# The second block's phase tables written one operation at a time along two loops, and lower halves of the down projection that alternate between VectorE and GpSimd

## The chip, the cores and the metric

The kernel runs on one core of a Trainium2 chip. The metric is the device time of one execution in microseconds. The kernel before took 1963.02 us (median of 3 runs, 1962.67 to 1963.16).

## What is computed

Two transformer-like blocks, one after the other, on a sequence of 256 tokens with 1024 features, all in float32. The first block has two layers. Each is a mixing part (three kinds of attention) and a gated MLP with a short convolution:

```python
def conv_gated_mlp(h, w_up, conv_w, conv_b, w_down):
    u = h @ w_up                      # 1024 -> 2 x 2816
    u = lax.conv_general_dilated(u, conv_w[:, None, :], window_strides=(1,),
                                 padding=[(CONV_WIDTH - 1, 0)], ...) + conv_b
    gate, val = jnp.split(u, 2, axis=-1)
    return (jax.nn.silu(gate) * val) @ w_down
```

The second block has a state space branch (a complex scan over time in 32 groups), a sparse attention, gates and a mixture of 16384 small experts:

```python
def second_block(x, ...):
    xn = rmsnorm(h, norm1_g[layer])
    proj = xn @ w_in[layer]
    y_ssm = s5_branch(u, a_re[layer], a_im[layer], log_dt[layer], ...)
    ...
```

The kernel does the complex scan as a real one, after turning each step by a phase. For that it needs tables of sine and cosine of phase times time, 16 groups of 128 states by 256 steps each. These are the phase tables of the title. Their argument depends on the weights alone, not on the sequence.

## The kernel before

**Split products.** A float32 product is done in three matmuls: each operand is split into an upper half (rounded to fp32r, `hh`, `wh`, `yh`, `ach`) and a lower half (the rest, `hl`, `wl`, `yl`, `acl`), and high x high, high x low and low x high are added in PSUM (`mm3`, line 468).

**Units of weights.** All weights come in units of 128 x 1024 float32, in one list `plan`, in the order of use. Unit i goes through `raw` (a transfer, issued from the SyncE queue), `wh` (ScalarE, line 845) and `wl` (VectorE, line 1121, or GpSimd, line 1709), each with six buffers in this part of the kernel. The transfer of unit i waits for the lower half of unit i - 6; the upper half waits for TensorE to be done with unit i - 6. Which engine writes a unit's lower half is decided by the list `lower` (lines 218 to 241). In the up projections it goes by threes, VectorE, VectorE, GpSimd ("ddp"), up to the sixth last of their units; the last five alternate. In the down projections the first 14 of 22 units are GpSimd's and the last 8 VectorE's.

**Order of the work.** Every engine has its own program, written out by hand (`pe`, `act`, `dve`, `pool`), and waits on the others by semaphores. `stream(i)`, called in each of them at the same places, does all units up to five beyond i. One layer's MLP is:

- the up loop, 22 steps. Step f has units 2f (gate half) and 2f + 1 (value half) of the up weights, 24 matmuls each, and one PSUM bank. All engines stream these two units, which means that ScalarE makes the upper halves of units 2f + 5 and 2f + 6 and VectorE or GpSimd their lower halves. Then ScalarE copies the gate half with scale and bias into a buffer of `att` (`cb`), VectorE adds the two shifted terms of the convolution (line 1138, two instructions of one element a cycle that read PSUM and `att`), ScalarE applies Silu and copies the value half, VectorE does that one's convolution, GpSimd multiplies the two (line 1714, att<-att), ScalarE rounds the previous product to `yh`, GpSimd writes its rest `yl`.
- the down loop, 22 units, 12 matmuls of 512 columns each: two groups of tokens by two halves of the output, in four banks that collect all 22. It needs y of f for unit f.

**Phase tables.** `phase_tables(L)` (line 1252) makes the arguments of half of the tables in each layer L, 4 pairs of groups by sine and cosine. VectorE calls it once, between the two loops (line 1402). It has 36 instructions on tiles of 128 x 512, all with operands in SBUF, each of them waiting for the one before: a product of time and frequency, for the cosine a quarter added, then the nearest integer found by adding and subtracting a large constant in a scratch tile `ptmp`, and subtracted. The scratch tile lies in `att`, in buffers of the convolution, so the function first waits for GpSimd's last `yl`. ScalarE turns the arguments into sines in later parts of the kernel.

```python
                for f in range(NTILE):
                    stream(first["wup", L] + 2 * f)
                    stream(first["wup", L] + 2 * f + 1)
                    ...
                phase_tables(L)
                for f, t in down_order:
                    if t:
                        stream(first["wdown", L] + f)
```

Of the kernel before, what the change touches and what calls it, by code (L numbers as in the profile page):

```python
# [26 lines left out]
NTILE = 22  # L27
# [61 lines left out]
def tcols(t):  # L89
    return slice(t * 128, (t + 1) * 128)  # L90
# [5 lines left out]
def program(nc, x_d, pos_d, consts_d, smalls_d, win_d, wout_d, wup_d, wdown_d, rows_d, wu_d, wqkv_d, wqk_d, wga_d, wsm_d,  # L96
            wglu_d, wsu_d, wau_d, wout2_d, wpq_d, keys_d, ut_d, vt_d, out_d, spill_d):
    with ExitStack() as ctx:

        def scoped(where, name, n, dt=F32):  # L100
            return where.enter_context(nc.sbuf_tensor(name, [128, n], dt))
# [17 lines left out]
        att = scoped(sc_l, "att", 3072)[:, :]  # L119
        headtmp = scoped(sc_l, "headtmp", 512)[:, :]  # L120
# [29 lines left out]
        def signal(name, step=1):  # L150
            return Signal(ctx.enter_context(nc.semaphore(name)), name, step)

        pe_out, act_out, dve_out, pool_out = [signal(n) for n in ("pe_out", "act_out", "dve_out", "pool_out")]
# [8 lines left out]
        plan, first = [], {}  # L162
# [54 lines left out]
        lower = []  # L217
        for i in range(n_units):
            d2 = first["wga"] - 8 <= i < first["wglu"] - 2
            if first["ut"] <= i < first["ut"] + J_GATE:  # L220
                lower.append("p")
            elif first["ut"] <= i < first["vt"]:
                lower.append("d")
            elif i >= first["ut"]:
                lower.append("dp"[i % 2])
            elif i >= first["wpq"]:
                lower.append("dp"[i % 2])
            elif i >= first["wglu"] - 2:
                lower.append("p")
            elif d2:  # L230
                lower.append("d")
            else:
                L = 0 if i < first["row", "n", 1] else 1
                if first["row", "n", L] + 7 <= i < first["wdown", L] - 5 and not (L == 0 and i < first["win", 0] + 6):
                    lower.append("ddp"[i % 3])
                elif first["wdown", L] <= i < first["wdown", L] + 14:
                    lower.append("p")
                elif first["wdown", L] + 14 <= i < first["wdown", L] + NTILE:
                    lower.append("d")
                else:  # L240
                    lower.append("dp"[i % 2])

        def raw_of(i):
            return raws[slot[i]][:, 0:plan[i][1]]

        def high_of(i):
            return whs[slot[i]][:, 0:plan[i][1]]

        def low_of(i):
            return wls[slot[i]][:, 0:plan[i][1]]  # L250
# [24 lines left out]
        def con(c, n):  # L275
            return con_s[:, c - 128:c - 128 + n]
# [136 lines left out]
        def ps(*item):  # L413
            return banks[bank_of[item]][:, :]

        def quad(bank, n=4):
            return bank[:, 0:n * 128].rearrange("p (k c) -> p k c", k=n)
# [694 lines left out]
        def dve(v):  # L1112
            at = [0]

            def stream(i):
                while at[0] <= until[i]:
                    u = at[0]
                    at[0] += 1
                    if plan[u][2] and lower[u] == "d":
                        v.wait_ge(act_hi, ("hi", u))  # L1120
                        v.e.tensor_tensor(low_of(u), raw_of(u), high_of(u).bitcast(F32), ALU.subtract).then_inc(dve_lo.up(("lo", u)), 1)  # L1121


            def tt(out, a, b, op, ev=None, alone=False):
                if not alone:
                    v.wait_ge(dve_out)
                v.e.tensor_tensor(out, a, b, op).then_inc(dve_out.up(ev), 1)  # L1127

            def ts(out, a, s1, s2, op0, op1, ev=None):
                v.wait_ge(dve_out)  # L1130
                if op1 is None:
                    v.e.tensor_scalar(out, a, s1, None, op0).then_inc(dve_out.up(ev), 1)  # L1132
                else:
                    v.e.tensor_scalar(out, a, s1, s2, op0, op1).then_inc(dve_out.up(ev), 1)

            def stt(out, a, s, b, op0, op1, ev=None):
                v.wait_ge(dve_out)
                v.e.scalar_tensor_tensor(out, a, s, b, op0, op1).then_inc(dve_out.up(ev), 1)  # L1138
# [23 lines left out]
            def halves_low(k0, n, cols, src, hi, ev):  # L1162
                v.wait_ge(act_out, hi)
                tt(hTl[:, k0:k0 + n, cols], src, hTh[:, k0:k0 + n, cols].bitcast(F32), ALU.subtract, ev, alone=True)

            def turned(st, ts_, nq, k_off=0):
                for t in ts_:
                    for q in range(nq):
                        halves_low(k_off + 4 * q, 4, tcols(t), quad(ps("T", st, t, q)), ("hTh", st, t, q), ("hT", st, t, q))
# [35 lines left out]
            def state_constants():  # L1205
# [43 lines left out]
                tt(kr, t16[1], t16[0], ALU.mult)  # L1249
                tt(ki, t16[2], t16[0], ALU.mult)  # L1250

            def phase_tables(L):
                ptmp = att[:, 0:512].rearrange("p (n t) -> p n t", n=2)
                tv = con(K_T, 256).unsqueeze(1).broadcast_to([128, 2, 256])
                v.wait_ge(pool_out, ("y", L, NTILE - 1))
                for n in range(8 * L, 8 * L + 8, 2):
                    fb = fr[:, n:n + 2].unsqueeze(2).broadcast_to([128, 2, 256])
                    for tab, quarter in ((sinT, 0.0), (cosT, 0.25)):
                        o = tab[:, n:n + 2, :]
                        tt(o, tv, fb, ALU.mult)  # L1260
                        if quarter:
                            ts(o, o, quarter, None, ALU.add, None)
                        ts(ptmp, o, MAGIC, None, ALU.add, None)
                        ts(ptmp, ptmp, MAGIC, None, ALU.subtract, None)
                        tt(o, o, ptmp, ALU.subtract, ("phase", L))

            def rope(u, half, cos, sin, tmp, ev):
                n = 2 * u.shape[2] * half
# [26 lines left out]
            def add_to_x(n, t, bank, ev):  # L1295
                tt(x[:, t, n * 512:(n + 1) * 512], x[:, t, n * 512:(n + 1) * 512], bank[:, :], ALU.add, ev, alone=True)
# [8 lines left out]
            for L in range(DEPTH):  # L1305
# [76 lines left out]
                for n in range(2):  # L1382
                    for h in range(4):
                        if h in (0, 3):
                            t = h // 3
# [4 lines left out]
                        stream(first["wout", L] + 4 * n + h)  # L1390
                stream(first["row", "f", L])
                turned(("f", L), (0, 1), 2)
                for f in range(NTILE):
                    stream(first["wup", L] + 2 * f)
                    stream(first["wup", L] + 2 * f + 1)
                    for half in range(2):
                        col, c = convs[L][:, f + NTILE * half, :], cb[f % 4][half]
                        bank = ps("up", L, f)[:, 256 * half:256 * half + 256]
                        v.wait_ge(act_out, ("c", L, f, half))
                        stt(c[:, 1:256], bank[:, 0:255], col[:, 1:2], c[:, 1:256], ALU.mult, ALU.add)  # L1400
                        stt(c[:, 2:256], bank[:, 0:254], col[:, 0:1], c[:, 2:256], ALU.mult, ALU.add, ("conv", L, f, half))
                phase_tables(L)
                for f, t in down_order:
                    if t:
                        stream(first["wdown", L] + f)
                    if f == NTILE - 1:
                        if t and L == 0:
                            turned(("n", 1), (0,), 2)
                        for n in range(2):
                            v.wait_ge(pe_out, ("down", L, t, n))  # L1410
                            add_to_x(n, t, ps("down", L, t, n), ("xd", L, t, n))
                        if L:
                            row = first["row", "g"]
                            v.wait_ge(act_out, ("sq", "g", t))
                            ts(ms[:, t:t + 1], ss[:, t:t + 1], 1.0 / 1024, EPS, ALU.mult, ALU.add, ("ms", "g", t))
                            v.wait_ge(pool_out, ("rs", "g", t))
                            v.wait_ge(slot_in[slot[row]], ("raw", row))
                            v.wait_ge(dve_out)
                            v.e.scalar_tensor_tensor(x[:, t, :], x[:, t, :], rstd[:, t:t + 1], raw_of(row), ALU.mult, ALU.mult
                                                     ).then_inc(dve_out.up(("gx", t), ("used", row) if t else None), 1)  # L1420
                            norm_scale(("n", 2), t, mix, first["row", "n", 2])
                        else:
                            norm_scale(("n", 1), t, mix, first["row", "n", 1])
# [117 lines left out]
            for c in range(20):  # L1541
# [4 lines left out]
                if c - 4 in (7, 15):  # L1546
                    t = (c - 4) // 8
# [9 lines left out]
            for n in range(2):  # L1557
                for h in range(4):
                    if h in (0, 3):
                        t = h // 3  # L1560
# [422 lines left out]
```

## Time and profile before

| | |
|---|---|
| median of 3 runs | 1963.02 us (1962.67 to 1963.16) |
| the profiled execution's own time | 1962.71 us |
| its span | 1960.6 us |
| mean granted clock of TensorE | 0.925 of full speed |
| busy: TensorE matmul / weight load | 91% / 79% |
| busy: VectorE / ScalarE / GpSimd | 65% / 44% / 40% |
| up loop, layer 0 / layer 1 (us of the span) | 206 to 333 / 591 to 718 |
| down loop, layer 0 / layer 1 | 333 to 405 / 718 to 793 |

The span is cut by the first and the last instruction of the profile. Engines in its rows are PE (TensorE), PEld (its weight loads), DVE (VectorE), ACT (ScalarE), POOL (GpSimd) and SP (SyncE). A row names a line of the kernel, the operation, and the tile written <- the tiles read. Numbers of buffers are left out, so `wl` stands for all six. A busy share is an average over the span; what a stage waits for must be read from that stage.

### The profile page before, as it was taken

How to read it: one execution, taken by the hardware profiler on the slowest of the kernel's cores; microseconds unless marked ns; L12 is line 12 of the kernel's file. 1: busy time of each engine (PE TensorE's matmuls, PEld its weight loads, DVE VectorE, ACT ScalarE, POOL GpSimd, SP SyncE). 2: the span in 40 equal slices, each digit the busy share in tenths (PEclk: the TensorE clock that was granted, in tenths of full speed). 3: DMA queues.
4: the chain of work that ended last, by engine and by line, in shares of the span. 5: the costliest groups of instructions: out<-in, count | busy, mean ns of one | idle time of the engine just before them, and what ended most of it. 6: DMA issues, size and time to landing. Idle time of an engine off the chain costs nothing.

```text
span 1960.6 us, 27291 instructions
## 1 busy us (share of the span) xinstructions
PE 1785.2 (91%) x10680; PEld 1555.1 (79%) x10680; DVE 1281.3 (65%) x2470; ACT 868.9 (44%) x1500; POOL 779.2 (40%) x410
## 2 busy tenths in 40 slices
PE   5999899789989997688889899789999999999997
PEld 4677899677669996555667799789999988888886
DVE  6653674954546758687763459998999944444444
ACT  5443565335336652412432344444444445555553
POOL 3211468432125683175633359770000014444443
PEclk9887899899789998788967899899999999999998
DMA  6421455444115554322321535454444456666664
GB/s 219 140 76 33 167 179 192 145 175 133 54 36 201 181 175 161 132 76 76 105 77 54 179 127 182 149 166 142 144 141 141 149 170 193 194 195 193 194 192 141
DMA packets 77311, 283.19 MB, mean 144 GB/s; under 512 B 8704, under 2 KB 8960, under 8 KB 76800
## 3 DMA queue, kind: packets, MB, share of 16 engines
q1 hardware_dynamic: 75888, 275.97, 43.3%
q10 hardware_dynamic: 1296, 5.49, 0.7%
q8 instruction: 84, 1.38, 0.3%
q14 instruction: 43, 0.35, 0.1%
HBM read 279.33 MB, written 2.10 MB: 144 GB/s over the span
## 4 chain that ended last, share of the span: by engine, by line
PE 64%; DVE 24%; ACT 4%; issue 4%; POOL 3%; DMA 1%; POOLq 0%; DVEq 0%; ACTq 0%
PE bank L468 52%; PE bank L459 9%; DVE wl L1121 4%; DVE tab L1127 2%; DVE H L1127 2%; ACT wh L845 2%; PE bank L551 2%; DVE att L1132 2%; DVE ssb L1127 1%; DVE att L1138 1%; DVE H L1586 1%; DVE H L1592 1%; DVE H L1588 1%; DVE H L1584 1%; DVE H L1590 1%
## 5 line engine op out<-in xcount | busy, mean ns | idle before, releaser
L1709 POOL TENSOR_TENSOR wl<-raw,wh 128x1024 fp32r<-128x1024 f32 x231 | 598.9, 2602 | 862.3 <-ACT wh L845 862.1
L845 ACT ACTIVATE wh<-raw 128x1024 fp32r<-128x1024 f32 x515 | 531.4, 1048 | 175.4 <-PE bank L468 166.0
L468 PE MATMUL bank<-hh,wh 128*128 128x256 f32 x1904 | 545.6, 287 | 18.6 <-DVE hl L1127 17.3
L468 PE MATMUL bank<-hl,wh 128*128 128x256 f32 x1904 | 538.1, 283 | 0.0
L468 PE MATMUL bank<-hh,wl 128*128 128x256 f32 x1904 | 536.8, 282 | 0.0
L1121 DVE TENSOR_TENSOR wl<-raw,wh 128x1024 fp32r<-128x1024 f32 x284 | 402.7, 1426 | 131.0 <-ACT wh L845 130.8
L468 PEld LDWEIGHTS bank<-hh,wh 128*128 128x128 f32 x1904 | 364.4, 191 | 20.9 <-issue 14.4
L468 PEld LDWEIGHTS bank<-hl,wh 128*128 128x128 f32 x1904 | 364.3, 191 | 0.0
L468 PEld LDWEIGHTS bank<-hh,wl 128*128 128x128 f32 x1904 | 363.8, 191 | 0.0
L1127 DVE TENSOR_TENSOR acl<-H,ach 128x256 fp32r<-128x256 f32 x128 | 87.6, 685 | 183.2 <-ACT ach L848 183.2
L468 PE MATMUL bank<-wh,ach 128*128 128x512 f32 x512 | 200.0, 391 | 1.9 <-DVE acl L1127 1.9
L468 PE MATMUL bank<-wl,ach 128*128 128x512 f32 x512 | 199.9, 390 | 0.0
L468 PE MATMUL bank<-wh,acl 128*128 128x512 f32 x512 | 199.7, 390 | 0.0
L468 PE MATMUL bank<-wh,hh 128*128 128x512 f32 (+1 forms) x432 | 184.3, 427 | 11.5 <-DVE hl L1127 6.6
L848 ACT ACTIVATE H<-bank 128x256 f32<-128x256 f32 (+33 forms) x193 | 63.8, 331 | 256.5 <-PE bank L468 224.0
L468 PE MATMUL bank<-wl,hh 128*128 128x512 f32 (+1 forms) x432 | 177.2, 410 | 0.0
L468 PE MATMUL bank<-wh,hl 128*128 128x512 f32 (+1 forms) x432 | 176.8, 409 | 0.0
L848 ACT ACTIVATE ach<-H 128x256 fp32r<-128x256 f32 x128 | 53.4, 418 | 174.3 <-PE bank L468 173.8
L1138 DVE SCALAR_TENSOR_TENSOR att<-bank,sml,att 128x255 f32<-128x255 f32 (+1 forms) x176 | 84.5, 480 | 64.0 <-ACT att L848 60.9
L468 PEld LDWEIGHTS bank<-wh,hh 128*128 128x128 f32 x432 | 88.1, 204 | 41.0 <-issue 15.2
L468 PEld LDWEIGHTS bank<-wh,ach 128*128 128x128 f32 x512 | 96.4, 188 | 22.3 <-issue 2.1
L468 PEld LDWEIGHTS bank<-wl,ach 128*128 128x128 f32 x512 | 96.5, 189 | 20.1
(183 smaller groups left out, 2439.5 us busy)
## 6 DMA issues: line engine op xcount, KB each, us to landing
raw<-in_ut_dram SPq DMA_DIRECT2D x128, 512.0 KB, 3.5
raw<-in_vt_dram SPq DMA_DIRECT2D x128, 512.0 KB, 3.6
raw<-in_wup_dram SPq DMA_DIRECT2D x88, 512.0 KB, 4.0
raw<-in_win_dram SPq DMA_DIRECT2D x48, 512.0 KB, 4.5
raw<-in_wdown_dram SPq DMA_DIRECT2D x44, 512.0 KB, 3.6
raw<-in_wout_dram SPq DMA_DIRECT2D x24, 512.0 KB, 3.5
raw<-in_wga_dram SPq DMA_DIRECT2D x16, 512.0 KB, 3.6
raw<-in_wpq_dram SPq DMA_DIRECT2D x16, 512.0 KB, 3.6
```

Source lines behind the costliest of these rows:

```text
L459: m = p.e.matmul(out, l, r, start=i == 0, stop=i == len(pairs) - 1)
L468: m = p.e.matmul(out, lhs[i][a], rhs[i][b], start=start and i == 0 and j == 0, stop=stop and i == n - 1 and j == 2)
L551: m = p.e.transpose(banks[b][:, 128 * k:128 * k + 128], buf[:, 1024 + 256 * (i % NB) + 128 * k:1152 + 256 * (i % NB) + 128 * k], ids[:, :])
L845: a.e.activation(high_of(u), raw_of(u), ACTF.Copy).then_inc(act_hi.up(("hi", u)), 1)
L848: a.e.activation(out, src, f, **kw).then_inc(act_out.up(ev), 1)
L1121: v.e.tensor_tensor(low_of(u), raw_of(u), high_of(u).bitcast(F32), ALU.subtract).then_inc(dve_lo.up(("lo", u)), 1)
L1127: v.e.tensor_tensor(out, a, b, op).then_inc(dve_out.up(ev), 1)
L1132: v.e.tensor_scalar(out, a, s1, None, op0).then_inc(dve_out.up(ev), 1)
L1138: v.e.scalar_tensor_tensor(out, a, s, b, op0, op1).then_inc(dve_out.up(ev), 1)
L1584: v.e.max(values[:, 0:8], s_).then_inc(dve_out.up(), 1)
L1586: v.e.max_index(index[:, 0:8], values[:, 0:8], s_).then_inc(dve_out.up(), 1)
L1709: g.e.tensor_tensor(low_of(u), raw_of(u), high_of(u).bitcast(F32), ALU.subtract).then_inc(pool_lo.up(("lo", u)), 1)
```

## The change

The 36 operations of `phase_tables` are no longer done in one call. The function becomes a generator that yields after each operation. The up loop takes one operation per step, after its two units are streamed and before the convolutions. The down loop takes two per unit after streaming it, so the 14 that are left are issued by f = 6. The scratch tile moves from `att` to `headtmp`, a tile that the attention part used before, and the wait for GpSimd's last `yl` is gone. The special rule for the down projection's lower halves is gone too: they now alternate between VectorE and GpSimd, as the general rule has it (the first down unit, an even index in `plan`, is VectorE's).

```diff
-                elif first["wdown", L] <= i < first["wdown", L] + 14:
-                    lower.append("p")
-                elif first["wdown", L] + 14 <= i < first["wdown", L] + NTILE:
-                    lower.append("d")
                 else:
                     lower.append("dp"[i % 2])
...
             def phase_tables(L):
-                ptmp = att[:, 0:512].rearrange("p (n t) -> p n t", n=2)
+                ptmp = headtmp.rearrange("p (n t) -> p n t", n=2)
                 tv = con(K_T, 256).unsqueeze(1).broadcast_to([128, 2, 256])
-                v.wait_ge(pool_out, ("y", L, NTILE - 1))
                 for n in range(8 * L, 8 * L + 8, 2):
                     fb = fr[:, n:n + 2].unsqueeze(2).broadcast_to([128, 2, 256])
                     for tab, quarter in ((sinT, 0.0), (cosT, 0.25)):
                         o = tab[:, n:n + 2, :]
                         tt(o, tv, fb, ALU.mult)
+                        yield
                         if quarter:
                             ts(o, o, quarter, None, ALU.add, None)
+                            yield
                         ts(ptmp, o, MAGIC, None, ALU.add, None)
+                        yield
                         ts(ptmp, ptmp, MAGIC, None, ALU.subtract, None)
+                        yield
                         tt(o, o, ptmp, ALU.subtract, ("phase", L))
+                        yield
...
+                tables = phase_tables(L)
                 for f in range(NTILE):
                     stream(first["wup", L] + 2 * f)
                     stream(first["wup", L] + 2 * f + 1)
+                    next(tables, None)
                     for half in range(2):
...
-                phase_tables(L)
                 for f, t in down_order:
                     if t:
                         stream(first["wdown", L] + f)
+                        next(tables, None)
+                        next(tables, None)
```

## Rows read from the trace of the kernel before

**Rows 1.** The page, part 1: busy time and share of TensorE.
```profile
PE 1785.2 (91%) x10680; PEld 1555.1 (79%) x10680; DVE 1281.3 (65%) x2470; ACT 868.9 (44%) x1500; POOL 779.2 (40%) x410
```
**Rows 2.** Waits of TensorE, down loop of layer 0, then layer 1: total, times, longest.
```profile
PE bank L468 <- DVE wl L1121: 11.8, 1, 11.8
...
PE bank L468 <- DVE wl L1121: 11.0, 1, 11.0
```
**Rows 3.** Stretches: length, TensorE busy (matmuls), granted clock, DMA share, GB/s.
```profile
383.86:387.50 3.64, 3.64 (x9) 0.50 0.57 192
768.06:773.20 5.14, 5.14 (x12) 0.50 0.71 231
391.20:402.00 10.80, 10.80 (x48) 1.00 0.54 206
436.00:518.00 82.00, 78.83 (x383) 1.00 0.41 126
```
**Rows 4.** Order of time on VectorE, down loop of layer 0: start, length, operation.
```profile
342.98 2.89 DVE L1127 TENSOR_TENSOR tab<-con,sta 128x512 f32<-128x512 f32 x1 [6.32 <-POOL yl L1714]
345.90 2.52 DVE L1132 TENSOR_SCALAR att<-tab 128x512 f32<-128x512 f32 x1
...
367.07 0.69 DVE L1127 TENSOR_TENSOR tab<-con,sta 128x512 f32<-128x512 f32 x1
367.79 0.43 DVE L1132 TENSOR_SCALAR att<-tab 128x512 f32<-128x512 f32 x1
...
382.58 6.89 DVE L1121 TENSOR_TENSOR wl<-raw,wh 128x1024 fp32r<-128x1024 f32 x6
```
**Rows 5.** Order of time on GpSimd, the same stretch.
```profile
342.90 23.58 POOL L1709 TENSOR_TENSOR wl<-raw,wh 128x1024 fp32r<-128x1024 f32 x9
```
**Rows 6.** Order of time on VectorE, up loop of layer 0, f = 9 to 12.
```profile
267.46 0.99 DVE L1138 SCALAR_TENSOR_TENSOR att<-bank,sml,att 128x255 f32<-128x255 f32 x2
...
271.59 1.64 DVE L1121 TENSOR_TENSOR wl<-raw,wh 128x1024 fp32r<-128x1024 f32 x1 [1.20 <-ACT wh L845]
273.15 0.99 DVE L1138 SCALAR_TENSOR_TENSOR att<-bank,sml,att 128x255 f32<-128x255 f32 x2
...
276.34 1.70 DVE L1121 TENSOR_TENSOR wl<-raw,wh 128x1024 fp32r<-128x1024 f32 x1 [0.25 <-ACT wh L845]
...
281.15 3.38 DVE L1121 TENSOR_TENSOR wl<-raw,wh 128x1024 fp32r<-128x1024 f32 x2 [0.26 <-ACT wh L845]
284.44 0.99 DVE L1138 SCALAR_TENSOR_TENSOR att<-bank,sml,att 128x255 f32<-128x255 f32 x2
```
**Rows 7.** Order of time on GpSimd, up loops: layer 0, then (last) layer 1.
```profile
272.11 3.39 POOL L1709 TENSOR_TENSOR wl<-raw,wh 128x1024 fp32r<-128x1024 f32 x1
...
277.10 1.53 POOL L1714 TENSOR_TENSOR yl<-att,yh 128x256 fp32r<-128x256 f32 x1
...
281.90 1.53 POOL L1714 TENSOR_TENSOR yl<-att,yh 128x256 fp32r<-128x256 f32 x1
...
661.92 3.40 POOL L1709 TENSOR_TENSOR wl<-raw,wh 128x1024 fp32r<-128x1024 f32 x1
```
**Rows 8.** Order of time on ScalarE, up loop of layer 0: Silu of f = 10.
```profile
274.18 0.42 ACT L848 ACTIVATE att<-att 128x256 f32<-128x256 f32 x1 [2.17 <-DVE att L1138]
```
**Rows 9.** Waits of ScalarE: layer 0's up loop (two rows), then layer 1's.
```profile
ACT att L848 <- DVE att L1138: 40.7, 20, 2.9
...
ACT att L848 <- PE bank L468: 2.9, 3, 1.7
...
ACT att L848 <- PE bank L468: 11.3, 15, 1.7
```
**Rows 10.** Stretches of the up loops, as in rows 3: matmuls up to a time.
```profile
206.00:279.05 73.05, 72.27 (x601) 0.97 0.52 182
591.00:669.84 78.84, 78.35 (x649) 0.97 0.55 186
600.00:714.00 114.00, 114.00 (x968) 1.00 0.53 178
```

## What the change is expected to do to the time

> **What bounds the kernel now.** I read the page first: TensorE is busy for 91% of the span [rows 1], so a change pays only where TensorE stands still. The waits of TensorE in the two down projections come next. There is one wait of size in each, 11.8 us in layer 0 and 11.0 us in layer 1, and both end with a lower half that VectorE writes [rows 2]. VectorE's order of time shows why [rows 4]: after the last convolution it idles 6.32 us for GpSimd, then it runs the 36 operations of `phase_tables` in one piece, from 342.98 to 382.6, and only then the lower halves that are its own by line 239. The first nine operations of the piece take 2.5 to 2.9 us each, the others 0.69 or 0.43 us. In the nine's time GpSimd runs nine lower halves without a gap, 23.58 us [rows 5]. So a table operation with its operands in SBUF that is issued while GpSimd is in a lower half waits for it to end.
>
> After each wait TensorE also works at half clock for a while: 9 matmuls in 3.64 us in layer 0 and 12 in 5.14 us in layer 1, at a granted 0.50 (1.2 GHz), against 48 in 10.80 us at 1.00 [rows 3], 0.225 us each. The loss is 3.64 - 9 x 0.225 = 1.6 us and 5.14 - 12 x 0.225 = 2.4 us.
>
> The up projections look idle by shares, but the order of time says otherwise. Each step f is a ring (units of weights are counted from 0 in each up projection, two to a step; a step makes the lower halves of units 2f+5 and 2f+6): ScalarE's two upper halves, VectorE's and GpSimd's lower halves, VectorE's convolution of the gate half, ScalarE's Silu, which waits for it, then the rest and the next upper halves. Three steps of this ring take 284.44 - 267.46 = 16.98 us between convolutions [rows 6]. TensorE's six units of weights take 6 x 24 x 114/968 = 17.0 us [rows 10]. The ring has no rate to spare. In layer 0 ScalarE waits for VectorE's convolutions 20 times, 40.7 us, and for TensorE only 2.9 us; in layer 1 for TensorE 11.3 us in 15 waits [rows 9]. What exists is a stock: in layer 0 unit 25's lower half (GpSimd's, first in program order at f = 10) ends at 272.11 + 3.39 = 275.50 [rows 7], and TensorE, after 25 units of 24 matmuls, starts it at 279.05 (601 matmuls by then, [rows 10]). The stock is 3.55 us. In layer 1 the same sum for unit 27 (649 matmuls at 669.84, its lower half ready at 661.92 + 3.40 = 665.32) gives 4.5 us [rows 7, 10].
>
> **The change, gains.** The piece of 36 operations leaves the point between the loops. VectorE no longer waits there for GpSimd's last y, and it can write its lower halves as their upper halves come. Both waits of TensorE and both half-clock stretches go: 11.8 + 11.0 + 1.6 + 2.4 = 26.8 us. What is late next is either TensorE itself or the ring above.
>
> **The change, costs in the up projections.** 22 of the 36 operations go one by one into the ring, behind VectorE's lower halves and ahead of the gate half's convolution. Queued behind it are both convolutions; Silu, GpSimd's product, ScalarE's y and the next upper halves wait for these. Without contention an operation costs 0.69 or 0.43 us [rows 4]; four of nine are of the long kind, so with 0.03 us between them it is 0.58 us on average. Whether GpSimd is in the way depends on who owns the two units of the step, which goes by threes ("ddp"):
> - GpSimd first, VectorE second (f = 10). VectorE's lower half ends at 271.59 + 1.64 = 273.23; GpSimd's has been queued since 272.11 and ends at 275.50, one undisturbed 2.36 us later [rows 6, 7]. The table operation is issued at 273.26 behind it and waits 2.26 us. Step longer by 2.26 + 0.58 = 2.84 us.
> - VectorE first, GpSimd second (f = 11). VectorE ends at 278.04, GpSimd's y, queued since 277.10, ends at 278.63 [rows 6, 7]. Longer by 0.6 + 0.58 = 1.2 us.
> - both VectorE's (f = 12). GpSimd's y at 281.90 ends at 283.43, inside VectorE's pair, which ends 284.53 [rows 6, 7]. GpSimd has nothing more. Longer by 0.6 us.
>
> That a queued GpSimd operation goes ahead of VectorE's next one, issued without a gap, is shown by that last pair: two lower halves take 3.38 us where six take 6.89 in the quiet stretch, 2.3 us for two [rows 4, 6]. The bounds of the wait in the first case are 0 (VectorE is served first, as it was at 271.59) and 2.36 us; I take 2.26, because the neighbouring rows show exactly the order of issue.
>
> In both layers the step f = 0 waits for the slow start of TensorE and hides its operation. Of steps 1 to 20 (the last whose delay reaches unit 47, the last but one lower half made here) 9 are of the first kind: every third, and after unit 38, where the halves alternate, each. Layer 0 has 5 of the second kind and 6 short ones, layer 1 about the same (step 1 counts as short, since GpSimd is idle there). That is 9 x 2.84 + 5 x 1.2 + 6 x 0.6 = 35.2 us in each layer. Less the stock, TensorE is later by 31.6 us in layer 0 and 30.7 us in layer 1.
>
> **Costs in the down projections.** The stock is now spent when they begin. Unit 49 needs the last operation of the up loop, two convolutions (2 x 1.0 us), two ScalarE steps, GpSimd's product, y's upper half, its own upper half (1.0) and a GpSimd lower half (2.4): about 9 us behind unit 47's, where TensorE takes 5.6 us for units 47 and 48: 3 us of wait. Then 14 table operations stand two to a unit. Each can meet one of GpSimd's halves, now every other unit. Up to unit 52 VectorE and GpSimd must take turns through four operations (2.3), two of VectorE's halves (2.3) and three or four of GpSimd's (7.1 to 9.4), 12 to 14 us, against some 8.4 us of TensorE's work from unit 49 to 51. From below it is nothing if GpSimd doesn't run ahead. I take 4 us, nearer the rows that show strict turns [rows 4, 5], so 7 us in each layer, with 0 and 10 as ends. The alternation of lower halves costs nothing by itself: GpSimd has 11 instead of 14, VectorE 11 of 1.15 us in about 60 us. The rest of the kernel sees its inputs later or earlier, and no order there changes. The scratch tile (now `headtmp`) is free by then, and ScalarE's two Sin calls find their tables done earlier than now.
>
> Sum: 31.6 + 30.7 + 2 x 7 - 26.8 = +49.5 us. Against the profiled execution, 1962.71 us (span 1960.6 us and 2.1 us around it), this is 2012.2 us; the median of the runs shown is 1963.02 us, 0.3 us above. I put 2012 us.
>
> The Trainium skill bears on this (SBUF — State Buffer, "Who interferes with whom"): the port pair that VectorE shares with GpSimd is an exclusive lock, held for the whole instruction, and the order of issue decides who blocks. By that rule the trace agrees, 2.5 to 2.9 us against 0.43 to 0.69. Had the two shared bandwidth instead, a table operation would cost perhaps double its 0.58 us, and the sum would stand near no change.
>
> **Rivals.**
> (a) The forecast: the ring in the up projections becomes the bound, through VectorE's waits for GpSimd. 0.66.
> (b) Faster: the operations don't wait in the first kind of step. This is the other side, decided at the moment VectorE's lower half ends: if VectorE's next operation is served before GpSimd's queued half, each step costs 0.6 us, 21 x 0.6 = 12.6 us in a layer, less 3.55 and 4.5 of stock: 17.2 - 26.8 = -9.6 us, 1953 us. For it: VectorE waits for nothing long between 271.59 and its end. Against it: the pair at 281.15. 0.12.
> (c) Faster: the ring has slack I don't see (ScalarE idles in every step), all operations are hidden and only the gain is left: 1936 us. Against it: the idle time of ScalarE ends with VectorE's convolution, which the operation pushes [rows 8]. 0.06.
> (d) Slower than forecast: the waits at the start of the down projections are long enough that the clock falls again, as after the present waits; twice 2 to 5 us, and the port turns cost their upper end, 2 x 3 us: about 2023 us. Against a fall inside the up projections: where TensorE has 383 matmuls in 82 us, it keeps a granted 1.00 [rows 3]. 0.13.
> (e) Costs and gains happen to cancel, within 0.2%: 0.03.
> That the change doesn't do what it says is not a case of its own: 22 + 44 calls exceed the 36 operations, so all are issued by f = 6 of the down projection.
>
> **How the numbers follow.** The likeliest case is (a), 2012 us. Its own range: the waits in the first kind of step half as long and no extra stall in the down projections give 2012 - 2 x 9 x 1.13 - 14 = 1978 us; upwards the ends of the down costs and the clock give 2025 to 2030 us. The range 1976 to 2030 us leaves out (b), (c) and (e) for the most part, 0.2 in all. 0.2% of the time, 3.9 us, is about what a measurement of this kernel can tell from no change. Faster 0.18, same 0.03, slower 0.79.
>
> **What would show it.** Right: three steps of the up ring take 21 to 22 us instead of 16.98; table operations of steps with GpSimd's unit first last 2.7 to 2.9 us, the others 0.4 to 1.3; TensorE waits for lower halves of GpSimd in the up projections, about 30 us a layer, and the waits of 11 us are gone. Wrong: ring periods near 17 us with table operations at 0.4 to 0.7 us (b, c). The weakest step is the order in which a queued GpSimd half and the table operation are served; next, what TensorE loses at the start of the down projections.

## The result and the profile after

The changed kernel takes 1990.63 us (median of 6 runs, 1987.65 to 2007.34) against 1962.85 us (6 runs, 1947.05 to 1971.12) for the kernel before. The ratio is 1.0184, with a 95% interval of 1.0145 to 1.0223; it isn't the quotient of the two medians, which is 1.0142. A second comparison, beside the experiments, gave 1.0255 (1.020 to 1.031). The profiled execution took 2006.87 us, 44.2 us more than the 1962.71 us of before.

The medians can't be compared to a few us, because in some executions the attention of layer 0 runs at half clock. It does so in seven of the twelve traces of this case, and in five, c_down's among them, it doesn't; the kernels all have the same program up to there. It costs 17 us: layer 0's first up matmul is at 206.78 us in the kernel before and at 189.96 us in c_down, a variant described further below. These are stretches of the two; the columns are length, TensorE busy (matmuls), granted clock, DMA share and GB/s.

```profile
140.00:160.00 20.00, 20.00 (x64) 0.50 0.00 0
```
```profile
140.00:160.00 20.00, 18.52 (x111) 1.00 0.00 1
```

The profiled executions of before and after both have the half clock there (x64 and x63), so these two are compared, and otherwise lengths of stages. No trace shows either of the two kernels without it; that some of their other executions ran so is inferred from their times. First the page of the changed kernel:

```profile
span 2005.1 us, 27289 instructions
PE 1805.5 (90%) x10680; PEld 1570.3 (78%) x10680; DVE 1324.6 (66%) x2476; ACT 865.6 (43%) x1500; POOL 774.5 (39%) x404
```

TensorE's busy time rose by 20 us [rows 1] though it has the same 10680 matmuls: part of them now run at half clock. The waits of TensorE, layer 0's MLP and then layer 1's, answer to rows 2:

```profile
PE bank L464 <- POOL wl L1713: 21.5, 9, 3.3
PE bank L464 <- DVE wl L1117: 2.2, 1, 2.2
...
PE bank L464 <- POOL wl L1713: 22.0, 10, 4.0
PE bank L464 <- DVE wl L1117: 0.9, 1, 0.9
```

The single waits of 11.8 and 11.0 us for VectorE are gone. In their place stand nine and ten waits, the longest 3.3 and 4.0 us, each for a lower half of GpSimd. How much later TensorE is, is seen from counts of matmuls. Unit 47 begins with the 1093rd of an MLP (44 up units of 24 and three down units of 12 come before it). First the kernel before (layer 0, then 1), then the changed one:

```profile
206.00:341.40 135.40, 134.62 (x1093) 0.99 0.54 182
591.00:726.30 135.30, 134.81 (x1093) 0.98 0.54 182
```
```profile
206.00:372.95 166.95, 146.15 (x1093) 0.92 0.43 145
615.00:778.35 163.35, 144.12 (x1093) 0.93 0.43 147
```

Unit 47 starts 31.3 us later in layer 0, and in layer 1, whose first up matmul is at 615.33 instead of 591.49, 28.1 us later. Why is seen in VectorE's order of time, f = 9 to 12 of layer 0 (in line with rows 6):

```profile
278.50 0.68 DVE L1123 TENSOR_TENSOR tab<-con,sta 128x512 f32<-128x512 f32 x1
279.28 1.00 DVE L1134 SCALAR_TENSOR_TENSOR att<-bank,sml,att 128x255 f32<-128x255 f32 x2
...
283.42 1.63 DVE L1117 TENSOR_TENSOR wl<-raw,wh 128x1024 fp32r<-128x1024 f32 x1 [1.20 <-ACT wh L841]
284.97 2.56 DVE L1128 TENSOR_SCALAR headtmp<-tab 128x512 f32<-128x512 f32 x1
287.64 1.00 DVE L1134 SCALAR_TENSOR_TENSOR att<-bank,sml,att 128x255 f32<-128x255 f32 x2
...
290.83 1.70 DVE L1117 TENSOR_TENSOR wl<-raw,wh 128x1024 fp32r<-128x1024 f32 x1 [0.25 <-ACT wh L841]
292.45 0.96 DVE L1128 TENSOR_SCALAR headtmp<-headtmp 128x512 f32<-128x512 f32 x1
293.51 1.00 DVE L1134 SCALAR_TENSOR_TENSOR att<-bank,sml,att 128x255 f32<-128x255 f32 x2
```

and in GpSimd's (in line with rows 7):

```profile
283.93 3.32 POOL L1713 TENSOR_TENSOR wl<-raw,wh 128x1024 fp32r<-128x1024 f32 x1
...
291.59 1.53 POOL L1718 TENSOR_TENSOR yl<-att,yh 128x256 fp32r<-128x256 f32 x1
```

At f = 10 the table operation is issued at 284.97, behind GpSimd's half, which has been queued since 283.93. It ends at 287.53, 0.3 us after that half's end at 287.25, and the convolution follows at 287.64. At f = 11 it waits only for a `yl` and takes 0.96 us; at f = 9, with nothing of GpSimd's in the way, 0.68 us. ScalarE's waits for the convolutions, 40.7 us before [rows 9], are now

```profile
ACT att L844 <- DVE att L1134: 78.4, 20, 5.2
```

37.7 us more. Read from the times at which the gate half's convolution starts, a step is longer by 2.7 to 3.0 us where GpSimd owns the first half, by 1.1 to 1.3 us where it owns the second, and by 0.5 to 0.8 us where it owns none. Of the last steps two in layer 0 and one in layer 1 show more, 3.4 to 3.8 us; up to 1.1 us of that stands in c_down too, which has no table operation there. Three steps take 21.3 to 21.9 us instead of 16.98.

### The profile page after: what moved, and what is told of

It reads as the page before. It is cut to its first block, busy times and chain, and to the rows that moved or that the text cites. A ratio compares the mean times of both kernels' runs of the same rounds, so it can differ in the third digit from the quotient of the medians.

```text
span 2005.1 us, 27289 instructions
## 1 busy us (share of the span) xinstructions
PE 1805.5 (90%) x10680; PEld 1570.3 (78%) x10680; DVE 1324.6 (66%) x2476; ACT 865.6 (43%) x1500; POOL 774.5 (39%) x404
## 4 chain that ended last, share of the span: by engine, by line
PE 58%; DVE 29%; ACT 7%; issue 3%; POOL 1%; DMA 1%; DVEq 0%; POOLq 0%; ACTq 0%
PE bank L464 46%; PE bank L455 9%; DVE wl L1117 8%; ACT wh L841 4%; DVE tab L1123 2%; DVE att L1134 2%; DVE H L1123 2%; PE bank L547 2%; DVE headtmp L1128 2%; ACT att L844 1%; DVE ssb L1123 1%; DVE H L1590 1%; DVE H L1596 1%; DVE H L1592 1%; DVE H L1594 1%
## 5 line engine op out<-in xcount | busy, mean ns | idle before, releaser
L1713 POOL TENSOR_TENSOR wl<-raw,wh 128x1024 fp32r<-128x1024 f32 x225 | 592.4, 2640 | 893.4 <-ACT wh L841 893.2
L464 PE MATMUL bank<-hh,wh 128*128 128x256 f32 x1904 | 553.8, 291 | 50.5 <-POOL wl L1713 33.1
L464 PE MATMUL bank<-hl,wh 128*128 128x256 f32 x1904 | 544.8, 286 | 0.0
L464 PE MATMUL bank<-hh,wl 128*128 128x256 f32 x1904 | 543.9, 286 | 0.0
L1117 DVE TENSOR_TENSOR wl<-raw,wh 128x1024 fp32r<-128x1024 f32 x290 | 420.3, 1455 | 151.1 <-ACT wh L841 150.9
L464 PEld LDWEIGHTS bank<-hh,wh 128*128 128x128 f32 x1904 | 372.1, 195 | 55.5 <-POOL wl L1713 40.6
L464 PEld LDWEIGHTS bank<-hl,wh 128*128 128x128 f32 x1904 | 371.9, 195 | 0.0
L464 PEld LDWEIGHTS bank<-hh,wl 128*128 128x128 f32 x1904 | 371.2, 195 | 0.0
```

The source lines that it names most:

```text
L464: m = p.e.matmul(out, lhs[i][a], rhs[i][b], start=start and i == 0 and j == 0, stop=stop and i == n - 1 and j == 2)
L1713: g.e.tensor_tensor(low_of(u), raw_of(u), high_of(u).bitcast(F32), ALU.subtract).then_inc(pool_lo.up(("lo", u)), 1)
```

## The experiments

All of them start from one of the two kernels; the edits are of VectorE's program and of the list `lower`. This table gives, counted in each trace from the first up matmul, how much later than before unit 47 starts, and the change of the whole MLP's length (before: 200.9 us and 201.1 us), layer 0 / layer 1; the length of three steps in the middle of the up loop; and the ratio to the kernel before.

| kernel | unit 47, us | MLP, us | three steps, us | ratio (95% interval) |
|---|---|---|---|---|
| before | | | 16.98 | |
| changed (x_after) | +31.1 / +28.0 | +23.5 / +20.5 | 21.3 to 21.9 | 1.0255 (1.020 to 1.031) |
| a_lower | +0.4 / -0.4 | +10.2 / +8.7 | | 1.0107 (1.0078 to 1.0136) |
| b_tables | +27.6 / +26.5 | +18.3 / +15.6 | | 1.0177 (1.0125 to 1.0229) |
| c_down | +0.5 / -0.1 | -13.1 / -13.7 | | 0.9867 (0.9819 to 0.9915) |
| d_down_dve | +0.4 / -0.6 | -13.3 / -14.2 | | 0.9823 (0.9762 to 0.9884) |
| f_second | +4.3 / +3.5 | -2.9 / -3.6 | 18.8 to 19.3 | 0.9923 (0.9883 to 0.9964) |
| g_quiet | +6.2 / +5.4 | -4.3 / -3.6 | 18.7 to 19.0 | 0.9970 (0.9941 to 1.0000) |
| e_between | +1.4 / +0.9 | -10.3 / -10.8 | 17.3 to 18.0 | 0.9869 (0.9818 to 0.9921) |
| j_psum | +12.9 / +11.9 | +3.4 / +2.4 | 19.3 to 19.4 | 1.0021 (0.9978 to 1.0065) |
| i_sbuf | +29.3 / +25.9 | +21.5 / +19.7 | 21.3 | 1.0220 (1.0155 to 1.0285) |

**The changed kernel again (x_after).**

> The changed kernel again, beside the others. My theory (operations that wait for GpSimd's queued halves lengthen the steps of the up loops): unit 47 starts some 28 to 32 us later than before, counted from the up loop's first matmul, in both layers; time 20 to 45 us above the kernel before. Rival (the profiled execution was an odd one and most executions lose much less in the up loops): unit 47 later by under 20 us, time less than 20 us above.

Unit 47 comes 31.1 and 28.0 us late, as in the first profile, and the median is 2000.94 us against 1947.84 us. The loss is no oddity of one execution. The rival falls.

**The two parts alone.** a_lower is the kernel before with the alternating lower halves:

```diff
-                elif first["wdown", L] <= i < first["wdown", L] + 14:
-                    lower.append("p")
-                elif first["wdown", L] + 14 <= i < first["wdown", L] + NTILE:
-                    lower.append("d")
```

> The kernel before with the alternating lower halves alone, tables still in one piece between the loops. Theory: unit 50 is now VectorE's and has to wait for the whole piece of 36 operations. The piece takes 21 us plus the rest of four of GpSimd's halves, about 30 us, so TensorE waits 20 to 23 us in each down loop where it waited 11 to 12, and the time is about 20 to 26 us above before. Rival (the alternation by itself is neutral, since GpSimd has fewer halves): TensorE's wait stays at 11 to 12 us and the time within 5 us of before.

TensorE waits 21.9 us in layer 0 (20.9 us in layer 1), and the median is 20.8 us above before. Its wait and VectorE's piece:

```profile
PE bank L464 <- DVE wl L1117: 21.9, 1, 21.9
```
```profile
324.47 2.89 DVE L1123 TENSOR_TENSOR tab<-con,sta 128x512 f32<-128x512 f32 x1 [2.67 <-POOL yl L1710]
...
353.60 3.49 DVE L1117 TENSOR_TENSOR wl<-raw,wh 128x1024 fp32r<-128x1024 f32 x3
```

The piece takes 29.1 us, four of its operations 2.5 to 2.9 us, and the next half of VectorE, which TensorE needs from unit 50 on, comes behind it. By itself the alternation hurts. It makes sense only once the piece is gone.

b_tables is the changed kernel with these four lines put back.

> The spread tables alone, with the old owners of the lower halves (14 of GpSimd, 8 of VectorE in the down loop). Theory: the up loops lose what they lose in the changed kernel, about 28 us a layer or a few us less, since the last two steps have no half of VectorE; the down loops lose little more, since VectorE owns nothing there before unit 58, but GpSimd must do a half per unit and each table operation delays it by 0.6 us: 2 to 5 us a layer. With the 27 us gained, 25 to 40 us above before. Rival (the alternation is what costs): near or below the time of before.

Unit 47 is 27.6 and 26.5 us late, the median 36.9 us above before. So the up loops lose nearly the same with either order of the down halves, and the spread tables are the cause of most of the loss. The alternation isn't free beside them, though: the two MLPs are 33.9 us longer than before here and 44.0 us in the changed kernel. The 10 us between them have arisen by unit 52.

**Out of the up loops (c_down).** All 36 operations go two to a unit into the down loops:

```diff
                     stream(first["wup", L] + 2 * f + 1)
-                    next(tables, None)
```

> The changed kernel with no table operation in the up loops; all 36 go two to a unit into the down loops, through unit 17. Theory: the steps of the up loops go back to 16.98 us for three, unit 47 starts when it did before, the stock of 3 to 6 us covers the turns at the port in the down loops, and the waits of 11 us are gone: 23 to 27 us below before, 1936 to 1940 us. Rival (the down loops are as sensitive as the up loops: VectorE and GpSimd need 5.9 us of port time for two units that TensorE does in 5.6): waits of TensorE of 5 us and more in each down loop, time within 15 us of before.

Three things were asked for and seen: unit 47 is back where it was, TensorE waits for no lower half in either down loop, and the two MLPs together are 26.8 us shorter than before, which is the gain of the prediction to a tenth. The median is 27.7 us below before (1920.14 us against 1947.84 us). The turns at the port are covered by the stock, but in layer 0 only just: VectorE's half of unit 52 ends at 338.59 us, and TensorE starts the unit at 338.97.

**All of the later halves VectorE's (d_down_dve).** c_down with

```diff
+                elif first["wdown", L] + 5 <= i < first["wdown", L] + NTILE:
+                    lower.append("d")
```

> All 36 table operations two to a unit in the down loops, and from unit 49 on all lower halves VectorE's. There is nothing of GpSimd's left for VectorE to wait for after the last y, and VectorE needs 1.2 + 2 x 0.58 us per unit where TensorE needs 2.8. Theory: TensorE waits for nothing in the down loops and the result is that of the variant with alternating halves or up to 5 us better, 25 to 32 us below the kernel before. Rival (VectorE alone falls behind at the entry, where five units stand ready): a wait of some us for a VectorE half, and no better than the alternating variant.

The MLPs are 27.5 us shorter than before, against 26.8 us in c_down: no difference that counts. TensorE is the bound in both. The ratios can't tell them apart either, since their intervals overlap.

**Same operations, another owner of the first half (f_second).** The number of GpSimd's halves in the loop stays, but where it has one it has the second of the step:

```diff
-                    lower.append("ddp"[i % 3])
+                    u = i - first["wup", L]
+                    lower.append("ddp"[i % 3] if u < 5 else "dddpdp"[(u - 5) % 6])
+                elif first["wdown", L] - 5 <= i < first["wdown", L] + 5:
+                    lower.append("pd"[i % 2])
```

> The changed kernel, but wherever GpSimd owns a half in the up loops from unit 5 on, it is the second of its step (per three steps: VectorE both, VectorE first, VectorE first; from unit 39 on VectorE first in each). Same operations, same number of halves for each engine. Theory: no step of the first kind is left, so a table operation waits for a y of GpSimd (0.6 us) and not for a half (2.26 us). Three steps take about 19 us instead of 21.6, and unit 47 or 48 starts 8 to 16 us later than before, not 28 to 31; time about 25 to 35 us below the changed kernel, near the kernel before. Rival (a table operation costs about 1.6 us whatever stands in GpSimd's queue): three steps at 21 us or more, time within 10 us of the changed kernel.

Three steps take 18.8 to 19.3 us, as expected, and no table operation of the up loops takes longer than 1.23 us. Two in a row with GpSimd's half second:

```profile
261.84 0.95 DVE L1131 TENSOR_SCALAR headtmp<-tab 128x512 f32<-128x512 f32 x1
...
267.71 0.97 DVE L1131 TENSOR_SCALAR headtmp<-headtmp 128x512 f32<-128x512 f32 x1
```

Unit 47, now VectorE's, is 4 us late and unit 49 8.2 and 7.3 us; in the changed kernel unit 49 is 34.8 and 31.5 us late. The gain over the changed kernel (50.7 us of the MLPs' length) is larger than the 25 to 35 us I expected. The step rate was right, but I had not counted two things. The new order has a larger stock: its half of GpSimd for unit 14 ends 6.0 us before TensorE starts that unit (layer 0), in the changed kernel the one for unit 13 only 1.1 us before. And two of three steps, and every step from unit 39 on, take 5.9 to 6.2 us, little above TensorE's 5.66 us.

**Three operations at once, where GpSimd is idle (g_quiet).**

```diff
-                    next(tables, None)
+                    if all(lower[first["wup", L] + 2 * f + k] == "d" for k in (5, 6)):
+                        for _ in range(3):
+                            next(tables, None)
```

> The changed kernel with its table operations in the up loops bunched: three in each step whose two halves are both VectorE's, none in the others (21 instead of 22 in the up loop). Theory: GpSimd has nothing queued at that point, so the three cost 3 x 0.58 us and three steps take 17 + 1.7 = 18.7 us instead of 21.6. Unit 47 starts 5 to 10 us later than before; time 35 to 45 us below the changed kernel, a little below the kernel before. Rival (it is the number of operations in the ring that counts, at 1.6 us each): time within 10 us of the changed kernel.

The up loop has 18 operations in this variant, not the 21 that I expected: six of its steps have two halves of VectorE's, and none of the last five does. That is four fewer than in the changed kernel. At the rival's 1.6 us each, 18 would cost 29 us, and unit 47 would be some 25 us late after the stock. It is 6.2 and 5.4 us late, instead of 31.3 and 28.1 us, and a later step with three operations is 1.7 to 2.0 us longer. VectorE's order of time at f = 9 of layer 0:

```profile
272.07 0.68 DVE L1123 TENSOR_TENSOR tab<-con,sta 128x512 f32<-128x512 f32 x1
272.78 0.43 DVE L1128 TENSOR_SCALAR headtmp<-tab 128x512 f32<-128x512 f32 x1
273.25 0.43 DVE L1128 TENSOR_SCALAR headtmp<-headtmp 128x512 f32<-128x512 f32 x1
```

Three operations cost less there than one behind a queued half.

**Between the two convolutions (e_between).**

```diff
-                    next(tables, None)
...
                         stt(c[:, 2:256], bank[:, 0:254], ...)
+                        if half == 0:
+                            next(tables, None)
```

> The changed kernel with the up loop's table operation moved behind the gate half's convolution, where VectorE idles 0.94 us for ScalarE's copy of the value half. Silu no longer waits for it. Theory: hidden in the steps whose halves are both VectorE's; in steps with GpSimd's half second the operation waits for that half and the value half's convolution comes 1.7 us late; with GpSimd's half first it comes 1 us late. About 2.8 us per three steps instead of 4.6: unit 47 12 to 18 us later than before, time 15 to 30 us below the changed kernel. Rival (the gate half's convolution is not what the ring turns on): no difference to the changed kernel.

The direction was right, the size wrong: unit 47 is 1.4 and 0.9 us late, not 12 to 18. Three steps take 17.3 to 18.0 us. At f = 10 and 11 of layer 0:

```profile
276.25 1.60 DVE L1128 TENSOR_SCALAR headtmp<-tab 128x512 f32<-128x512 f32 x1
277.95 1.00 DVE L1134 SCALAR_TENSOR_TENSOR att<-bank,sml,att 128x255 f32<-128x255 f32 x2
...
281.03 0.81 DVE L1128 TENSOR_SCALAR headtmp<-headtmp 128x512 f32<-128x512 f32 x1
```

I had let the operation at f = 11 wait for a whole half of GpSimd. But GpSimd's product and `yl` wait for the value half's convolution, which is now a little later, and its half stands in the queue behind them: it starts at 281.51, when VectorE's operation has been issued (at 281.03). And a value half's convolution that comes 0.8 us late delays neither Silu nor ScalarE's next upper halves. The ring turns on the gate half's convolution, and that one no longer waits.

**The wait apart from the operation (j_psum and i_sbuf).** Both are c_down with one extra VectorE operation per step (in j_psum from f = 1 on), without use, where the changed kernel has its table operation. It has the same shape, 128 x 512, and one operand, in PSUM (j_psum, the first) or in SBUF (i_sbuf, the second):

```diff
+                    if f:
+                        ts(headtmp, ps("up", L, f - 1), 1.0, None, ALU.mult, None)
...
+                    ts(headtmp, headtmp, 1.0, None, ALU.mult, None)
```

In j_psum TensorE also waits for one operation more before it takes the bank back:

```diff
-                    emptied[b] = (dve_out, ("conv", L, f, 1))
+                    emptied[b] = (dve_out, ("conv", L, f + 1, 0) if f + 1 < NTILE else ("conv", L, f, 1))
```

> The counterpart of the variant with an extra SBUF operation: all 36 table operations in the down loops, and in each step of the up loops but the first an extra VectorE operation of the same shape (128 x 512, one operand) at the place of the table operation. This one reads the PSUM bank of the step before, so only its result goes to SBUF; TensorE gets that bank one operation later, eight steps ahead of its next use. Theory: it waits for nothing, takes 0.6 to 0.7 us in every kind of step although it is the longer one, three steps take 18.8 to 19.1 us against 21.3 with the SBUF operand, and unit 47 starts 5 to 10 us later than before; time 30 us or more below the variant with the SBUF operand. Rival (whatever stands ahead of the gate half's convolution costs that much): three steps 21 us and more, unit 47 later by 25 us and more.

> The same, but the extra operation reads the scratch tile in SBUF instead of PSUM (one operand, 0.43 us undisturbed, shorter than the other's). Theory: it waits for GpSimd as the table operations did, 2.2 us where GpSimd has the first half and 0.6 us where it has the second. Three steps take 21.2 us and unit 47 starts 25 to 30 us later than before; time 30 us and more above the variant with the PSUM operand. Rival (the port is no part of it): like the PSUM variant or faster, since the operation is shorter.

First j_psum, then i_sbuf, each a step with GpSimd's half first and the one behind it:

```profile
263.74 0.68 DVE L1128 TENSOR_SCALAR headtmp<-bank 128x512 f32<-128x512 f32 x1
...
269.34 0.68 DVE L1128 TENSOR_SCALAR headtmp<-bank 128x512 f32<-128x512 f32 x1
```
```profile
262.99 2.56 DVE L1128 TENSOR_SCALAR headtmp<-headtmp 128x512 f32<-128x512 f32 x1
...
270.46 0.95 DVE L1128 TENSOR_SCALAR headtmp<-headtmp 128x512 f32<-128x512 f32 x1
...
278.02 0.42 DVE L1128 TENSOR_SCALAR headtmp<-headtmp 128x512 f32<-128x512 f32 x1
```

The operation with the PSUM operand is the slower one when nothing is in the way, 0.68 us against 0.42 us, and takes 0.68 us in every kind of step. The one with the SBUF operand takes 2.56, 0.95 and 0.42 us, as the table operations do. Three steps take 19.4 against 21.3 us, unit 47 is 12.9 and 11.9 us late against 29.3 and 25.9 us, and the medians are 1965.54 and 1998.07 us, from comparisons with kernels before of 1960.89 and 1951.15 us. The extra operation differs in its operand alone. The other two differences don't explain the gap: TensorE shows no wait for a bank in j_psum, and the operation at f = 0 that it lacks takes 0.42 us in i_sbuf. In j_psum the lateness is 2 to 3 us above the upper end of what I expected: a step is longer by 0.79 us, the operation and 0.1 us around it, where I had put 0.6 to 0.7.

## Why the prediction was right, step by step

- **The gain**, 26.8 us, is what c_down shows when the operations are out of the way and the alternation is in: 13.1 and 13.7 us. That the tenths agree is chance. In the changed kernel itself, TensorE's way from unit 52 to the end of the down loop is 13.5 us shorter in each layer. The half-clock stretches behind the old waits were part of the gain, as counted.
- **The ring has no rate to spare.** Shown by the changed kernel (three steps 21.3 to 21.9 us, predicted 21 to 22) and from the other side by c_down, where they go back.
- **The kinds of steps**: predicted 2.84, 1.2 and 0.6 us, measured 2.7 to 3.0, 1.1 to 1.3 and 0.5 to 0.8 us. The order of service, which I called the weakest step, is as the pair of halves in rows 6 had it: what is queued first goes first. f_second, g_quiet and the last pair of experiments each take away the wait and leave the work; rival (b)'s price, 0.6 us a step, is near what j_psum pays everywhere, 0.79 us.
- **Unit 47**: predicted 31.6 and 30.7 us late, measured 31.3 and 28.1 us. Layer 1 is 2.6 us less: its step f = 2, counted as one with a wait, had none (0.97 us for the operation), since GpSimd's half came later there.
- **The entry of the down loops**: predicted 3 us for unit 49 and 4 us for the turns at the port, 7 us a layer. Unit 49 is 34.8 and 31.5 us late, 3.5 and 3.4 us more than unit 47. Unit 52 is 2.5 us later still in both layers (in layer 1, 1.4 us of it from unit 50 on). That makes 6 us: the entry cost half a us more than predicted and the turns 1.5 us less. The turns themselves are as predicted, one table operation to one of GpSimd's halves. First GpSimd's row, four halves without a gap, then VectorE's rows, of which the last is unit 52's half. It ends at 392.59, and TensorE starts the unit at 392.64:

```profile
379.37 10.81 POOL L1713 TENSOR_TENSOR wl<-raw,wh 128x1024 fp32r<-128x1024 f32 x4
...
382.75 2.62 DVE L1128 TENSOR_SCALAR headtmp<-tab 128x512 f32<-128x512 f32 x1
385.40 2.51 DVE L1128 TENSOR_SCALAR headtmp<-headtmp 128x512 f32<-128x512 f32 x1
387.95 2.78 DVE L1123 TENSOR_TENSOR tab<-tab,headtmp 128x512 f32<-128x512 f32 x1
390.76 0.69 DVE L1123 TENSOR_TENSOR tab<-con,sta 128x512 f32<-128x512 f32 x1
391.37 1.22 DVE L1117 TENSOR_TENSOR wl<-raw,wh 128x1024 fp32r<-128x1024 f32 x1
```

- **The alternation**: the prediction had it costing nothing by itself, which holds in c_down, where TensorE waits for no lower half, but not elsewhere. With the tables in one piece it costs 21 us (a_lower). Beside the spread tables the MLPs are 10 us longer with it than without it (44.0 against 33.9 us in b_tables). Part of these 10 us is in the prediction under other names: its count of steps and its turns at the port both go by alternating owners. So the sum did not suffer by the whole of them; how much each part has isn't shown.
- **The sum**: the MLPs are 23.7 and 20.5 us longer, 44.2 us, which is also the whole difference of the two profiled executions; predicted was 49.5 us. The 5 us are layer 1's step (2.6 us) and the entries of the down loops (2 x 1 us) for the most part.
- **2012 us** was 21 us above the median. 5 us of this are the sum. The rest is the level: I started from an execution with half clock in the attention of layer 0, as the three runs shown all were by their times, and of the six runs of the changed kernel two had 2007 us and four 1988 to 1992 us. Compared with like executions, 1962.7 and 2007 us, the difference is 44 us.
- **Rival (d)** and its row: I had argued from rows 3 that the clock wouldn't fall inside the up loops. It does, see below. As far as these traces show it costs nothing there, because the ring and not TensorE sets the pace: in layer 0 TensorE starts each unit whose half GpSimd makes first in its step, from unit 19 to unit 49, 0.1 us after that half has ended.

The Trainium skill's rule (SBUF — State Buffer, "Who interferes with whom") is borne out in three points by these runs: the wait lasts to the end of GpSimd's instruction (2.56 us for an operation of 0.42 us), the order of issue decides who waits, and an instruction of VectorE with at most one SBUF input, outside the modes that use two ports, does not contend (the one whose only input is in PSUM takes 0.68 us in each kind of step).

## What to carry to other kernels

An idle share of an engine says nothing about room in a loop of several engines: add up one turn of the ring, here 16.98 us for three steps against TensorE's 17.0, before anything is put into it, and find the instruction on which it turns. If work must go in, put it where the ring doesn't wait for it (behind the gate half's convolution, 0.2 us a step instead of 1.5), or where the other user of the port has nothing queued, or into a stage in which the bound engine has stock. Try the parts of a change apart and in other places: the alternation alone costs 21 us and the spreading alone 37 us, but the alternation with the tables in the down loops gains 27 us, and c_down or d_down_dve is the version to keep. Whether the tables in the down loops need the alternation is open, since no variant has them there with the old owners.

## What the runs showed of the hardware

TensorE's clock fell inside the up loops of the changed kernel, although it is kept at 1.00 through the projections with 383 matmuls in 82 us [rows 3]. These stretches of layer 0 lie around and behind waits of 2 to 3.3 us for GpSimd's halves; the columns are those of rows 3:

```profile
264.60:271.50 6.90, 5.96 (x28) 0.51 0.47 152
287.40:291.80 4.40, 4.40 (x25) 0.62 0.69 242
330.40:336.30 5.90, 5.90 (x28) 0.51 0.53 178
```

28 matmuls of 256 columns take 5.9 us at 1.2 GHz, where the loop has 8.5 in 1 us at 2.4 GHz [rows 10]. So the waits understate what was lost: in layer 0 they sum to 23.7 us up to unit 52, which is 37.3 us late. The lateness has to be read from a count of matmuls, not from the waits.
